# Holding back the weight queue of a decoder step until the small vectors, the identity and x have landed

## The chip, the cores and the metric

The kernel runs on one core of one Trainium2 chip. The metric is the device time of one execution in microseconds (us). Three runs of the kernel before gave 1500.31, 1504.12 and 1505.19 us; the median is 1504.12 us. Each run comes from the same inputs.

## The reference

One decoder layer is computed for a prompt of 256 tokens and for 8 single-token samples, model width 1024, all in 32-bit floats. Cut to what matters:

```
m = silu(c) @ w_mod + b_mod                        # c: 9 vectors; w_mod 1024 x 6144
sh1, sc1, gt1, sh2, sc2, gt2 = split(m, 6)
h = rmsnorm(x, g_pre_mix) * (1 + sc1) + sh1
aq, af, ai, ag, bq, bk, bv, gate_a, gate_b = split(h @ w_in)    # w_in 1024 x 5632
o_a = hgrn2(aq, af, ai, ag)                        # 4 heads, 128x128 state
o_b = differential_attention(bq, bk, bv)           # 4 heads, paged cache for the samples
merged = sigmoid(gate_a) * (o_a @ w_proj_a) + sigmoid(gate_b) * (o_b @ w_proj_b)
x = x + gt1 * rmsnorm(merged @ w_out, g_post_mix)
h2 = rmsnorm(x, g_pre_ffn) * (1 + sc2) + sh2
x = x + gt2 * rmsnorm(moe(h2), g_post_ffn)         # top 4 of 32 experts, 12 MB of weights each
```

## The kernel before, in words

The engines run programs of their own, written out in order by hand and tied together by semaphores. Three of them issue DMAs, each on a queue of its own.

SyncE issues nearly all weights, in the order of the list `UNITS`: 54 pieces of 1 MB that pass through a ring of four slots (tile `ring`). The first eight are pieces of `w_mod` for the first third of the modulation (`("mod", 0, k)`); then each half of a 512-column block of `w_in` is followed by two more `w_mod` pieces for as long as there are any; the branch and output projections come last. Before piece n, from the fifth on, SyncE waits until the piece that had the same slot is used (`after_unit`, L300 to L322). After the ring it issues the weights of expert 0, and then loops over the other experts, twelve pieces each, into the ring and the tile `late`.

ScalarE begins (L890 to L914) by issuing seven small vectors into `vrows` and the 128x128 identity into the head of `cst` (eight DMAs, semaphore `small_loaded`), and then the two parts of x (`x_loaded`, 32 when both are in). It then takes a sigmoid of the conditioning vectors once they are transposed, waits for x, squares its three chunks with a row sum, takes a root and an exponential, and only then issues the rest of the constants table (`cst`, semaphore `cst_loaded`), which is first used in the attention.

GpSimd issues biases, post-norm gains, lambdas and router weights (17 DMAs, L355 to L369), and later the pages of the cache.

TensorE waits for `small_loaded`, transposes `vrows` (`vt`, L455), and VectorE makes silu(c) from it (`cT`, L1120). Then `mod_part` (L466) multiplies the ring pieces as they land, four matmuls in 32-row strips for each piece's 2048 columns (eight instructions in the trace). After the eighth, VectorE adds the bias, four transposes bring the result into columns (`mt0`), and eight rounds follow in which TensorE transposes a 128-column block of the normalised x (`xt0` to `xt7`, L452) and VectorE scales and shifts it into `hT` (L1092). After the last round the first input projection starts (`in_T(4)`, L496). The projections, the two token mixers, the output projection and the router follow, and from about 455 us the loop over experts (L828, L847, L869), for which the weights stream in behind.

Of the kernel before, what the change touches and what calls it, by code (L numbers as in the profile page):

```python
# [132 lines left out]
def build(nc, a, o):  # L133

    ctx = ExitStack()
    with ctx:
# [5 lines left out]
        def S(name):  # L142

            if name not in sems:
                sems[name] = ctx.enter_context(nc.semaphore(name))
            return sems[name]
# [126 lines left out]
        def slot(i):  # L273

            return ring[:, i * SLOT:(i + 1) * SLOT] if i < 4 else late[:, (i - 4) * SLOT:(i - 3) * SLOT]
# [6 lines left out]
        def after_unit(n):  # L282

            u = UNITS[n]
            if u[0] == "mod":
                return "mod_used", KC * u[1] + u[2] + 1
            if u[0] == "in":
                names = IN_NAMES[u[1]]
                if u[2] == 1:
                    return "proj_full", PROJ[names[-1]] + 1  # L290
                return ("proj_full", PROJ[names[1]] + 1) if len(names) == 4 else ("tok_half", 1 if u[1] == 6 else 2)
            if u[0] in ("pb", "pa"):
                return "merge_full", (KC if u[0] == "pa" else 0) + 4 * (u[1] + 1)
            return "yo_full", 2
# [4 lines left out]
        @block.sync  # L299
        def _(sp):  # L300
            wmod = a["w_mod"][0].rearrange("(k p) n -> p k n", p=P)
            win = a["w_in"][0].rearrange("(k p) n -> p k n", p=P)
            for n, u in enumerate(UNITS):
                if n >= 4:
                    sem, value = after_unit(n - 4)
                    sp.wait_ge(S(sem), value)
                dst = slot(n % 4)
                if u[0] == "mod":
                    src = wmod[:, u[2], u[1] * 2048:(u[1] + 1) * 2048]
                elif u[0] == "in":  # L310
                    src = win[:, :, u[1] * 512 + u[2] * 256:u[1] * 512 + (u[2] + 1) * 256]
                    dst = dst.rearrange("p (k n) -> p k n", k=KC)
                elif u[0] in ("pa", "pb"):
                    w = a["w_proj_a" if u[0] == "pa" else "w_proj_b"][0].rearrange("(h p) n -> p h n", p=P)
                    src = w[:, :, u[1] * 512:(u[1] + 1) * 512]
                    dst = dst.rearrange("p (h n) -> p h n", h=H)
                else:
                    src = a["w_out"][0, u[1] * 256:(u[1] + 1) * 256, :].rearrange("(k p) n -> p k n", p=P)
                    dst = dst.rearrange("p (k n) -> p k n", k=2)
                sp.dma_start(dst, src).then_inc(S(f"piece{n % 4}_landed"), 16)  # L320

            def load_expert(e, u):  # L322
                one = slice(e, e + 1) if isinstance(e, int) else bass.ds(e, 1)
                if u < 8:
                    src = a["w_gate_up"][0, one, u * P:(u + 1) * P, :]
                    src = src.rearrange("e p n -> p (e n)")
                    dst = slot(u)
                else:
                    src = a["w_down"][0, one, (u - 8) * 2 * P:(u - 7) * 2 * P, :]
                    src = src.rearrange("e (k p) n -> p (e k) n", p=P)  # L330
                    dst = slot(u).rearrange("p (k n) -> p k n", k=2)
                sp.dma_start(dst, src).then_inc(S(f"w{u}_landed"), 16)  # L332


            sp.wait_ge(S("merge_full"), 2 * KC)
            sp.wait_ge(S("st_stored"), 16)
            for h in range(2):
                sp.wait_ge(S(f"s0_{h}_stored"), 32)
            for u in range(4, 12):
                load_expert(0, u)  # L340
            sp.wait_ge(S("yo_full"), 2)
            for u in range(4):
                load_expert(0, u)
            sp.wait_ge(S("tab_ready"), 1)
            with sp.Fori(1, E) as e:
                before = sp.value_load(used_tab[0:1, bass.ds(e, 1)], min_val=0, max_val=12 * MAXB)
                for u in range(12):

                    sp.wait_ge(S("w_used"), before + (u + 1))
                    load_expert(e, u)  # L350
# [1271 lines left out]
```

## Time and profile before

| | |
|---|---|
| runs | 1500.31, 1504.12, 1505.19 us |
| median | 1504.12 us |
| span of the profiled execution, first to last instruction | 1499.4 us (no other time of that execution is on record) |
| TensorE matmul busy | 1331.5 us, 89% |
| VectorE / ScalarE / GpSimd busy | 390.1 / 196.2 / 56.7 us |
| mean granted TensorE clock | 0.943 |
| DMA | 496.16 MB, mean 331 GB/s |
| share of the SyncE queue (q1) / GpSimd queue (q0) / ScalarE queue (q10) | 76.4% / 4.6% / 2.5% of 16 engines |

Busy time is the time in which an engine executed something; the queue shares are the time of their packets as a part of what the 16 DMA engines have over the span. The granted clock is a part of TensorE's full speed.

### The profile page before, as it was taken

Reading aid. Unit: us, or ns where it says so; the run is one execution under the profiler, and the core shown is the slowest. Engines: PE = TensorE matmul, PEld = TensorE weight load, DVE = VectorE, ACT = ScalarE, POOL = GpSimd, SP = SyncE. Lnnn points to the kernel's source line nnn. Section 1 sums busy time; section 2 is a strip of 40 time slices with the busy share of each in tenths; the row PEclk is TensorE's granted clock in tenths of the full one; section 3 lists DMA queues with packets and bytes.
Section 4 is the critical chain, followed back from the end, with each engine's and each line's share of the span. In section 5 each row is a group of like instructions: output and inputs, shape, how many; then the busy total and the mean of one; then the engine's idle time right before and its main releaser. Section 6 shows DMA issues by size and latency. Waiting matters only on the chain.

```text
span 1499.4 us, 18873 instructions
## 1 busy us (share of the span) xinstructions
PE 1331.5 (89%) x6987; PEld 716.6 (48%) x6988; DVE 390.1 (26%) x653; ACT 196.2 (13%) x321; POOL 56.7 (4%) x108
## 2 busy tenths in 40 slices
PE   2999999998868999999899998999999999989980
PEld 0576778876444544544344333544543443334430
DVE  1713652355353211211122111211211121112105
ACT  2001410011121111111011110110110111101111
POOL 2001011100000000000000000000000000000003
PEclk9798999799976999999999999999999999999995
DMA  9888475322721999999999999799999999999974
GB/s 304 299 297 282 140 256 165 119 108 91 280 112 66 397 419 417 417 419 418 419 416 419 418 419 417 293 394 417 419 419 419 416 418 419 420 417 417 419 290 144
DMA packets 114980, 496.16 MB, mean 331 GB/s; under 512 B 9461, under 2 KB 32234, under 8 KB 78954
## 3 DMA queue, kind: packets, MB, share of 16 engines
q1 hardware_dynamic: 101216, 459.30, 76.4%
q0 software_dynamic: 6832, 23.09, 4.6%
q10 hardware_dynamic: 6906, 13.42, 2.5%
q8 instruction: 16, 0.26, 0.1%
q14 instruction: 10, 0.08, 0.0%
HBM read 478.41 MB, written 17.37 MB: 331 GB/s over the span
## 4 chain that ended last, share of the span: by engine, by line
PE 54%; DMA 24%; SPq 12%; DVE 5%; ACT 2%; issue 2%; ACTq 0%; POOL 0%; DVEq 0%; POOLq 0%
DMA late<-in_w_gate_up 21%; PE PB L847 13%; SPq L332 11%; PE PB L869 9%; PE PB L828 8%; PE PB L496 8%; PE PB L513 2%; PE PB L758 2%; PE PB L725 2%; PE PB L466 1%; PE PB L678 1%; PE PB L452 1%; PE PB L521 1%; DMA cst<-in_consts 1%; DVE wide L1099 1%
## 5 line engine op out<-in xcount | busy, mean ns | idle before, releaser
L847 PE MATMUL PB<-late,gates 128*64 128x512 f32 x1056 | 245.5, 598 | 37.8 <-DMA late<-in_w_gate_up 37.8
L869 PE MATMUL PB<-late,gates 128*64 128x512 f32 x1056 | 233.9, 595 | 24.1 <-ACT gates L1046 24.1
L847 PE MATMUL PB<-ring,gates 128*64 128x512 f32 x1056 | 233.6, 595 | 0.3 <-issue 0.3
L1570 DVE TENSOR_SCALAR gates<-PB 128x512 f32<-128x512 f32 x33 | 22.8, 692 | 740.8 <-PE PB L854 740.8
L828 PE MATMUL PB<-gates,wide 128*128 128x64 f32 x1632 | 194.3, 280 | 6.9 <-DVE gates L1542 6.9
L828 PEld LDWEIGHTS PB<-gates,wide 128*128 128x128 f32 x1632 | 189.7, 196 | 20.6 <-issue 20.6
L847 PEld LDWEIGHTS PB<-late,gates 128*64 128x64 f32 x1056 | 69.3, 136 | 208.3 <-issue 104.5
L496 PE MATMUL PB<-hT,ring 128*128 128x264 f32 x576 | 149.6, 418 | 2.6 <-DVEq L1157 2.2
L869 PEld LDWEIGHTS PB<-late,gates 128*64 128x64 f32 x1056 | 72.9, 137 | 163.9 <-issue 131.9
L847 PEld LDWEIGHTS PB<-ring,gates 128*64 128x64 f32 x1056 | 76.0, 138 | 147.6 <-issue 145.2
L496 PEld LDWEIGHTS PB<-hT,ring 128*128 128x128 f32 x576 | 116.7, 207 | 34.4 <-issue 8.9
L1042 ACT ACTIVATE gates<-gates 128x512 f32<-128x512 f32 x33 | 20.8, 630 | 434.9 <-DVE gates L1570 434.9
L1566 DVE TENSOR_REDUCE gates<-att 128x192 f32<-128x768 f32 x33 | 48.8, 1478 | 50.9 <-PE PB L828 50.9
L1049 ACT ACTIVATE gates<-PB 128x512 f32<-128x512 f32 x33 | 19.7, 597 | 246.8 <-PE PB L876 246.8
L1042 ACT ACT_TABLE_LOAD x33 | 42.3, 1283 | 52.6 <-issue 52.6
L421 POOL CAST sel<-cst 96x64 bf16 x31 | 7.2, 233 | 958.8 <-PE PB L876 958.8
L1044 ACT ACTIVATE gates<-PB 128x512 f32<-128x512 f32 x33 | 19.7, 597 | 133.7 <-PE PB L828 133.7
L466 PE MATMUL PB<-ring,cT 128*32 128x512 f32 x192 | 29.4, 734 | 8.2 <-DMA ring<-in_w_mod 6.5
L725 PE MATMUL PB<-late,ring 128*128 128x264 f32 x128 | 30.8, 403 | 4.3 <-DVE gates L1096 4.3
L1563 DVE TENSOR_TENSOR att<-cst,small 128x768 f32<-128x768 f32 x33 | 31.6, 958 | 1.1
L513 PE MATMUL PB<-ring,hT 128*128 128x256 f32 x128 | 30.8, 396 | 0.0
L725 PEld LDWEIGHTS PB<-late,ring 128*128 128x128 f32 x128 | 25.3, 199 | 10.4 <-issue 5.6
(260 smaller groups left out, 850.1 us busy)
## 6 DMA issues: line engine op xcount, KB each, us to landing
late<-in_w_gate_up SPq DMA_DIRECT2D x128, 1024.0 KB, 23.1
late<-in_w_down SPq DMA_DIRECT2D x128, 1024.0 KB, 22.1
ring<-in_w_gate_up SPq DMA_DIRECT2D x128, 1024.0 KB, 18.7
ring<-in_w_mod SPq DMA_DIRECT2D x24, 1024.0 KB, 7.0
ring<-in_w_in SPq DMA_DIRECT2D x22, 1024.0 KB, 8.5
ybuf<-gates ACTq DMA_DIRECT2D x66, 128.0 KB, 6.2
wide<-in_cache_k POOLq DMA_DIRECT2D x16, 256.0 KB, 3.3
G<-in_cache_v POOLq DMA_DIRECT2D x16, 256.0 KB, 3.0
```

The source lines that it names most:

```text
L332: sp.dma_start(dst, src).then_inc(S(f"w{u}_landed"), 16)
L466: mm = pe.matmul(PB[4][32 * j:32 * j + 32, :], cT[:, k, :], w[:, j * 512:(j + 1) * 512], start=(k == 0), stop=(k == KC - 1))
L496: mm = pe.matmul(bank[:, 0:T], w[:, k * 256 + (j % 2) * P:k * 256 + (j % 2 + 1) * P], hT[:, k, :], start=(k == 0), stop=(k == KC - 1))
L513: mm = pe.matmul(banks[c][:, half * 256:(half + 1) * 256], hT[:, k, c * P:(c + 1) * P], w[:, k * 256:(k + 1) * 256], start=(k == 0), stop= ...
L725: mm = pe.matmul(PB[i % 4][:, 0:T], w[:, h * 512 + (s % 4) * P:h * 512 + (s % 4 + 1) * P], src[:, h, :], start=(h == 0), stop=(h == H - 1))
L758: mm = pe.matmul(PB[2 * c + i][:, :], gaT[:, s, c * P:(c + 1) * P], wo[s // 2][:, (s % 2) * D + i * 512:(s % 2) * D + (i + 1) * 512], star ...
L828: mm = pe.matmul(PB[3][:, k * M:(k + 1) * M], xn[:, c, k * P:(k + 1) * P], mo["Pm"][:, c * M:(c + 1) * M], start=(c == 0), stop=(c == NCH ...
L847: mm = pe.matmul(PB[i][64 * half:64 * half + 64, :], mo["xT"][:, k * M:(k + 1) * M], slot(k)[:, i * D + half * 512:i * D + (half + 1) * 51 ...
L869: mm = pe.matmul(PB[2][64 * half:64 * half + 64, :], mo["actT"][:, (k % 4) * P + (k // 4) * M:(k % 4) * P + (k // 4) * M + M], slot(8 + k ...
L1042: act.activation(mo["sig"], mo["glu"], ACT.Sigmoid, scale=ALPHA).then_inc(S("sig_ready"), 1)
L1563: dve.tensor_tensor(eq3, iota, g3, ALU.is_equal).then_inc(S("eq_ready"), 1)
L1566: dve.tensor_reduce(P3, eq_sum, AX, ALU.add).then_inc(S("P_ready"), 1)
```

## The change

SyncE gets two waits. Before its first piece it waits for all eight small transfers of ScalarE's queue (seven vectors and the identity), and before its third piece for both parts of x. Order, sizes and destinations of all DMAs stay as they were.

```
         def _(sp):
             wmod = a["w_mod"][0].rearrange("(k p) n -> p k n", p=P)
             win = a["w_in"][0].rearrange("(k p) n -> p k n", p=P)
+            sp.wait_ge(S("small_loaded"), 16 * 8)
             for n, u in enumerate(UNITS):
+                if n == 2:
+                    sp.wait_ge(S("x_loaded"), 32)
                 if n >= 4:
                     sem, value = after_unit(n - 4)
                     sp.wait_ge(S(sem), value)
```

## Rows read from the trace of the kernel before

**Rows 1.** Chain of waits in order of time: start us, us, what.
```profile
4.66 14.82 DMA cst<-in_consts
21.63 5.27 PE PB L466 x32
26.92 11.53 DMA ring<-in_w_mod
51.01 9.63 PE PB L496 x32
```
**Rows 2.** Windows: length, busy (instructions) of five engines, clock, DMA share, GB/s.
```profile
5.00:10.00 5.00, 0.00 (x0) 0.00 (x0) 0.00 (x0) 1.28 (x1) 5.00 (x10) 1.00 1.00 330
20.00:25.00 5.00, 3.37 (x20) 0.83 (x24) 1.05 (x5) 0.26 (x1) 0.00 (x0) 1.00 1.03 255
35.00:40.00 5.00, 3.81 (x20) 0.40 (x16) 0.69 (x1) 0.00 (x0) 0.00 (x0) 0.50 1.03 407
450.00:480.00 30.00, 22.76 (x86) 15.77 (x87) 12.81 (x36) 4.10 (x9) 0.23 (x1) 0.52 0.01 2
```
**Rows 3.** Waits of TensorE, 51 to 460 us: total us, times, longest.
```profile
PE PB L496 <- DMA ring<-in_w_in: 0.4, 1, 0.4
PE PB L751 <- DMA ring<-in_w_out: 5.1, 1, 5.1
```
**Rows 4.** Timeline of TensorE and VectorE after the eighth piece: start us, us.
```profile
38.49 1.94 PE L466 MATMUL PB<-ring,cT 128*32 128x512 f32 x8 [0.64 <-DMA ring<-in_w_mod]
49.78 0.55 DVE L1092 TENSOR_SCALAR hT<-PB,A,SH 128x256 f32<-128x256 f32 x1 [0.15 <-DVE hT L1096]
```
**Rows 5.** DMA issues: KB each, median us to landing.
```profile
ring<-in_w_mod SPq DMA_DIRECT2D x1, 1024.0 KB, 5.2
wide<-in_cache_k POOLq DMA_DIRECT2D x4, 256.0 KB, 3.1
```
**Rows 6.** Timeline of the ScalarE and GpSimd issues.
```profile
4.66 0.36 ACTq L899 DMA_DIRECT2D cst<-in_consts  x1
5.05 0.50 ACTq L900 DMA_DIRECT2D x<-in_x_prompt  x1
10.40 0.61 POOL L369 DMA_DIRECT2D br<-in_b_router  x1
27.93 1.06 ACT L909 ACTIVATE hT<-x 128x1024 f32<-128x1024 f32 x1 [7.16 <-DMA x<-in_x_sample]
34.60 0.35 ACTq L914 DMA_DIRECT2D cst<-in_consts  x1
```
**Rows 7.** DMA queues, 0 to 9 us: packets, MB, share of 16 engines.
```profile
q1 hardware_dynamic: 277, 2.10, 65.2%
q0 software_dynamic: 94, 0.22, 10.8%
```
**Rows 8.** DMA queues, 0 to 38.5 us.
```profile
q1 hardware_dynamic: 1511, 8.76, 65.0%
q0 software_dynamic: 720, 1.72, 18.5%
q10 hardware_dynamic: 602, 1.37, 13.7%
```
**Rows 9.** DMA queues, 30 to 38.5 us.
```profile
q1 hardware_dynamic: 778, 3.37, 97.2%
q10 hardware_dynamic: 16, 0.18, 5.6%
```
**Rows 10.** TensorE on weight pieces: timeline, then windows (busy, clock, DMA share, GB/s).
```profile
30.94 1.26 PE L466 MATMUL PB<-ring,cT 128*32 128x512 f32 x8 [4.09 <-DMA ring<-in_w_mod]
33.43 1.93 PE L466 MATMUL PB<-ring,cT 128*32 128x512 f32 x8 [1.23 <-DMA ring<-in_w_mod]
22.00:24.00 2.00, 2.00 (x12) 1.00 0.99 238
24.00:25.00 1.00, 1.00 (x12) 1.00 1.05 221
```
**Rows 11.** Timeline of the second half of the first projection (the first: rows 1).
```profile
62.42 7.39 PE L496 MATMUL PB<-hT,ring 128*128 128x264 f32 x32
```

More of the change, by code:

```diff
@@ L302, in _ @@
             win = a["w_in"][0].rearrange("(k p) n -> p k n", p=P)
+            sp.wait_ge(S("small_loaded"), 16 * 8)
             for n, u in enumerate(UNITS):
+                if n == 2:
+                    sp.wait_ge(S("x_loaded"), 32)
                 if n >= 4:
```

## The prediction

> **What bounds the kernel now.** I read the chain of waits first, from its start. It opens with a wait for the identity matrix, issued at 4.66 us and landed 14.82 us later; then the first four weight pieces are multiplied in one go (5.27 us), then 11.53 us go to weight pieces that land one by one until 38.45 us, and the first projection starts at 51.01 us [rows 1]. The windows table comes second: between 5 and 50 us the DMA share is 1.00 to 1.04 in each of nine stretches of 5 us (three of them stand), so the DMA engines have no free moment there, and TensorE is busy 3.37 us of 5 at 20 to 25 us and 3.81 of 5 at 35 to 40 us [rows 2]. So what sets the time of the eighth weight piece (T7, 38.45 us) is the sum of all packets that pass before it. The early wait for the identity costs TensorE 19.5 us of idleness, and TensorE isn't what is short. From T7 to 51.01 us lie 12.6 us of a fixed sequence: eight matmuls (1.94 us), the bias, four transposes, and eight rounds of transpose and modulation at 0.9 us each on VectorE, the last starting at 49.78 us [rows 4]. From 51 us to the expert loop TensorE's matmuls wait for DMA only twice, 0.4 and 5.1 us (the second for the output weights, whose issue itself waits for TensorE) [rows 3], and at 450 to 480 us the DMA engines stand idle (share 0.01) with the first expert's weights all loaded [rows 2]. A shift of T7 therefore runs through to the end with its full size, in either direction, and no DMA lead absorbs it. My sum is: end = time before + shift of T7 + what the clock does.
>
> **The first wait: when the queue starts.** Before, the first piece was issued at 0.91 us and landed 5.2 us later [rows 5]. After, SyncE stands at its wait with all 54 ring pieces and the expert weights behind it. The last of the eight small transfers, the identity, is issued at 4.66 us [rows 6]. How long it then takes without weights in the way no row shows. From below stand 3.1 us, what 256 KB of cache keys took [rows 5]; from above the 14.82 us of now. I take 3.4, near the lower end, since what it competes with is only GpSimd's queue: small_loaded at about 8, the first weight byte at about 9 instead of 1.9, the first piece at some 14. The second wait, for x (issued at 5.05 us [rows 6], 1 MB), ends at 11 to 12 us; pieces 0 and 1 hold 2 MB, 5 us of traffic from 9 us on, so the third piece is queued before they are through and this wait costs nothing. If x came after 14 us, each us later would cost one.
>
> **Engine time lost while the queue waits.** In the first 9 us the weight queue used 65.2% of the DMA engines, 5.9 us of their time [rows 7]. Those 5.9 us are lost altogether if nothing else can use them, and not lost at all if the other two queues fill them. What they have to fill them with: up to 38.5 us GpSimd's queue takes 18.5%, 7.1 us for 1.72 MB (242 GB/s while it runs), and ScalarE's 13.7%, 5.3 us [rows 8]. GpSimd issues its 1.72 MB until 11.0 us [rows 6], about 180 GB/s on offer, so three quarters of the engines' time from some 3.4 us; from 6 us x fills the rest. That leaves 1.9 to 3.4 us empty and a quarter of 3.4 to 6: 2.2 us lost. Bounds 0 and 5.9.
>
> **What is drawn ahead of T7.** This is the term that I think counts most. The big constants table (1374.5 KB) is issued by ScalarE at 34.60 us, behind x (first square at 27.93 us) and 6.67 us of squares, a root, an exponential and two table loads [rows 6]. By 38.5 us only 0.18 MB of ScalarE's queue since 30 us has passed [rows 9], so nearly all of the table is moved while TensorE and VectorE are in the 12.6 us that follow T7, where DMA isn't needed. With x landed at 11 to 12 us the same steps put the issue at about 19 us, well ahead of T7, and the queues share the engines. 1.41 MB less 0.18 is 1.23 MB; at the rate of the weight queue when it is nearly alone (3.37 MB in 97.2% of 8.5 us, 408 GB/s [rows 9]) that is 3.0 us more before T7. In return the projection weights come that much earlier after T7, and nobody waits for them there. Bounds: 3.0, and 0 if some wait kept the table behind T7, for which I see no cause.
>
> **What less mixing gives back.** Before T7 the weight queue needs 65.0% of 38.5 us, 25.0 us, for 8.76 MB; at 408 GB/s it would be 21.5 [rows 8, 9]. So mixing with the small packets costs it 3.5 us, spread over some 23 us. Now most small traffic passes before the weights or beside the first three, so I take 2.0 of these 3.5 back. x and the small packets may also run faster without weights beside them: at 408 GB/s their 12.4 us for 3.09 MB would be 7.6, so at most 4.8 come back, but small packets are likely slow by themselves (242 GB/s above), so I take 0.8, near the end that changes nothing.
>
> **Sum.** T7 moves by 2.2 + 3.0 - 2.0 - 0.8 = +2.4 us, to about 40.9. From the bounds: 0 + 3.0 - 3.5 - 4.8 = -5.3 (-8.3 if the table too stayed behind T7), and 5.9 + 3.0 - 0 - 0 = +8.9.
>
> **TensorE earlier, and its clock.** The first matmul of the weights moves from 21.63 to some 14 us, worth nothing while T7 is set by DMA: pieces land 2.5 us apart and need 1.94 us at the slow rate [rows 4, 10]. Ring slots come free in time: piece 4 needs piece 0 used, at 16 us. The back-to-back run of 5.2 us, in which the matmuls came to double their rate (12 in 2.00 us from 22 to 24 us, 12 in 1.00 us from 24 to 25 [rows 10]), disappears. Before, it bought nothing: after the idle 4 us the next eight were still fast (1.26 us), the later ones slow (1.93, 1.94) [rows 4, 10], and the granted clock reads 0.50 (1.2 GHz) at 35 to 40 us [rows 2]. Even spacing should end in the same state, so 0. If the clock were high at T7, the last piece saves 1.0 and the first projection 2.2 (9.63 against 7.39 us [rows 1, 11]); the modulation rounds are VectorE's and save nothing: -3.2 at best.
>
> The profiled span is 1499.4 us and the median of the runs 1504.12, so 4.7 us lie around or between executions; none of the change touches these, so I add +2.4 to the median: 1506.5 us.
>
> **What the Trainium skill says against it.** The trace shows first that the identity, 64 KB, took 14.82 us next to the weight stream [rows 1]. "DMA: Bandwidth & Descriptors", section Rules for kernel authors, advises to issue a DMA early and to wait on its semaphore late, so that setup overlaps. By that rule the 7 us of later start would be lost in full, about 1511; by the rows above other queues fill most of them. It is near the slower rival below, which is priced from rows alone.
>
> **The rivals.** A difference of less than 0.3% (4.5 us) can't be told from none here.
> - Slower: the other queues can't use the engines while SyncE waits. What speaks for it: in the first 9 us GpSimd's queue moved only 0.22 MB (10.8% [rows 7]), perhaps because it is slow to start and not because weights were in its way. Then 5.9 are lost, the table costs 3.0, and 2.0 come back with less mixing: +6.9, 1511 us. It decides from the point where the engines stand empty over 4.3 us in total. Chance 0.24.
> - Faster: mixing was the real price, all 3.5 us of the weights and 4 of x and the small packets come back and the clock is high at T7: 2.2 + 3.0 - 3.5 - 4 - 3.2 = -5.5, 1498.6. For it: 255 GB/s at 20 to 25 us against 407 at 35 to 40 [rows 2]. Against it: small packets keep their cost wherever they stand. Chance 0.10.
> - Nothing happens: T7 within 1 us of 38.45 because the DMA queue is only reordered; 1504. A part of my case, as both read as no change.
> - The waits don't delay as said, small_loaded still coming near 19 us because GpSimd's packets and x hold the identity back: all would be late by 10 us. ScalarE's queue sends the identity ahead of x, so I give this 0.01, in slower.
>
> **The numbers.** Forecast 0.65 with its mirror case, slower 0.25, faster 0.10. Time 1506.5; the range reaches up to the slower rival's price and ends below at -3 us, and leaves about 1 in 10 out on either side: 1501 to 1511.
>
> **What would show it.** Right: identity landed near 8 us and the first transpose just behind it; first weight matmul at 13 to 15; the table issued at 18 to 20; DMA share under 0.8 at 0 to 5 us and 1.0 from 6 us on; T7 at 40 to 42; projection 12.6 us later; expert loop shifted by as much. Wrong: T7 below 38 with a rate over 350 GB/s between 10 and 30 us (mixing was underrated); T7 over 43 (engines empty); a table that passes after T7; a granted clock of 1.00 at the first projection.

## The result and the profile after

Over 20 runs each, the changed kernel has a median of 1508.59 us (1501.41 to 1513.06) and the kernel before 1502.39 us (1496.69 to 1508.69). The ratio is 1.0033 with a 95% interval of 1.0019 to 1.0047: slower by 5.0 us, between 2.9 and 7.1. (The ratio is an estimate from all the runs with its interval, and not the quotient of the two medians, which lie 6.2 us apart. Where a gain or loss of the whole kernel is given in us below, it is worked out from such a ratio.) That is on the edge of what I had called no difference; its sign is clear, and it is the sign of the forecast (+2.4 us).

The span of the profiled execution is 1506.6 us. The chain of waits of the kernel after, in order of time (start us, us, what):

```profile
4.92 11.68 DMA x<-in_x_sample
16.99 13.12 DMA ring<-in_w_mod
32.15 9.67 DMA ring<-in_w_mod
41.87 1.98 PE PB L469 x8
54.38 9.39 PE PB L499 x32
```

Against [rows 1], the wait for the identity is gone from the head, and a wait for x and 22.8 us of waits for weight pieces stand there. That the chain passes through x doesn't yet make the wait for x a cause; the first run below takes it out. The eighth piece lands at 41.82 us instead of 38.45 (the end of the second wait for pieces; T7, +3.37 us), and the first projection starts at 54.38 instead of 51.01 us, again +3.37. The 12.6 us between the two are the same.

The timeline of the kernel after has the steps that the prediction dated:

```profile
8.11 0.43 PE L455 MATMUL PB<-cst,vrows 101*128 101x101 f32 x1 [8.11 <-DMA cst<-in_consts]
16.68 1.06 ACT L912 ACTIVATE hT<-x 128x1024 f32<-128x1024 f32 x1 [7.31 <-DMA x<-in_x_sample]
19.74 1.93 PE L469 MATMUL PB<-ring,cT 128*32 128x512 f32 x8 [11.20 <-DMA ring<-in_w_mod]
23.34 0.35 ACTq L917 DMA_DIRECT2D cst<-in_consts  x1
```

The vectors are there at 8.1 us (predicted 8), but x only at 16.7 (11 to 12), the first weight matmul runs at 19.74 (14), and the table is issued at 23.34 (19) instead of 34.60 [rows 6]. TensorE got only 1.9 us of head start out of this, and used none of it. Two more of the listed signs failed: the DMA share is 0.89 at 5 to 10 us, not 1.0 from 6 us on (windows below), and the expert loop doesn't start 3.4 us later but 6.6, as the two timelines of its first matmul say, before and after:

```profile
460.56 10.48 PE L828 MATMUL PB<-gates,wide 128*128 128x64 f32 x48 [6.92 <-DVE gates L1542]
```
```profile
467.19 8.13 PE L831 MATMUL PB<-gates,wide 128*128 128x64 f32 x37 [6.93 <-DVE gates L1545]
```

I come back to this below.

The windows of the kernel after, with the columns of [rows 2]; then the first 5 us of the kernel before:

```profile
0.00:5.00 5.00, 0.00 (x0) 0.01 (x1) 1.48 (x5) 0.00 (x0) 3.75 (x12) 1.00 0.23 65
5.00:10.00 5.00, 0.43 (x1) 0.18 (x1) 0.88 (x5) 1.55 (x2) 5.00 (x10) 1.00 0.89 238
20.00:25.00 5.00, 3.40 (x16) 0.20 (x8) 2.42 (x4) 3.26 (x6) 0.00 (x0) 1.00 1.02 365
35.00:40.00 5.00, 3.60 (x24) 0.36 (x16) 0.00 (x0) 0.00 (x0) 0.00 (x0) 1.00 1.01 421
```
```profile
0.00:5.00 5.00, 0.00 (x0) 0.01 (x1) 1.48 (x5) 0.00 (x0) 3.75 (x12) 1.00 0.60 204
```

The DMA share (last but one) is where the empty time is read. Before, 2.0 us of the first 10 are empty (5 x 0.40, and none from 5 to 10); after, 5 x 0.77 + 5 x 0.11 = 4.4. So 2.4 us were lost by this count, with 2.2 predicted.

The DMA queues of the kernel after, first 38.5 us (packets, MB, share of 16 engines):

```profile
q1 hardware_dynamic: 1040, 7.62, 53.0%
q10 hardware_dynamic: 730, 2.61, 20.0%
q0 software_dynamic: 720, 1.72, 16.9%
```

ScalarE's queue has moved 2.61 MB by then against 1.37 [rows 8]: the 1.24 MB of difference are the table, all of it now ahead of T7, and the weight queue is 1.14 MB behind, about one weight piece.

### The profile page after: what moved, and what is told of

Its sections match the earlier page's. It is cut to its first block, busy times and chain, and to the rows that moved or that the text cites. A ratio compares the mean times of both kernels' runs of the same rounds, so it can differ in the third digit from the quotient of the medians.

```text
span 1506.6 us, 18873 instructions
## 1 busy us (share of the span) xinstructions
PE 1336.4 (89%) x6987; PEld 717.2 (48%) x6988; DVE 390.0 (26%) x653; ACT 196.2 (13%) x321; POOL 57.2 (4%) x108
## 4 chain that ended last, share of the span: by engine, by line
PE 56%; DMA 23%; SPq 12%; DVE 5%; ACT 2%; issue 2%; ACTq 0%; POOL 0%; DVEq 0%; POOLq 0%
DMA late<-in_w_gate_up 19%; PE PB L850 13%; SPq L335 11%; PE PB L872 9%; PE PB L831 9%; PE PB L499 9%; PE PB L516 2%; PE PB L761 2%; PE PB L728 2%; DMA ring<-in_w_mod 2%; PE PB L681 1%; PE PB L469 1%; PE PB L524 1%; PE PB L455 1%; DVE wide L1102 1%
## 5 line engine op out<-in xcount | busy, mean ns | idle before, releaser
L1573 DVE TENSOR_SCALAR gates<-PB 128x512 f32<-128x512 f32 x33 | 22.8, 692 | 741.0 <-PE PB L857 741.0
L499 PE MATMUL PB<-hT,ring 128*128 128x264 f32 x576 | 152.8, 425 | 2.8 <-DVEq L1160 2.2
L1045 ACT ACT_TABLE_LOAD x33 | 42.3, 1283 | 52.7 <-issue 52.7
```

Of the source, the lines that this page charges most:

```text
L499: mm = pe.matmul(bank[:, 0:T], w[:, k * 256 + (j % 2) * P:k * 256 + (j % 2 + 1) * P], hT[:, k, :], start=(k == 0), stop=(k == KC - 1))
L1045: act.activation(mo["sig"], mo["glu"], ACT.Sigmoid, scale=ALPHA).then_inc(S("sig_ready"), 1)
```

## The experiments

My theory after the result: T7 is a sum of DMA engine time, and the delay is 2.4 us of empty engines, plus 3.0 for the table, less some 2.0 given back by less mixing (packets of several queues passing side by side). The rivals put it down to the empty engines alone or to one of the waits. For each run the time is the ratio to the kernel before on the same chip (12 runs against 35, 95% interval). T7 comes from one profile each: the landing that released the last group of eight weight matmuls, which I give by the start of that group. Before it is 38.49 [rows 4], in the changed kernel 41.87.

### One wait at a time

The first wait alone:

```
+            sp.wait_ge(S("small_loaded"), 16 * 8)
             for n, u in enumerate(UNITS):
```

> Theory (T7 is the sum of engine time: about 2.4 us left empty while the queue waits, 3.0 us for a constants table drawn ahead of T7, less about 2 us given back by less mixing): the first wait alone does the whole of this, because all four first pieces then follow it and the DMA engines stay full. Identity landed near 8.1 us, T7 at 41.3 to 42.5, median 3 to 4 us over before. Rival (the second wait makes the delay, since the third piece is held until 16.6 us): T7 back at 38.5 to 39.5 and no difference of the medians.

Timeline of TensorE, last group:

```profile
41.83 1.56 PE L467 MATMUL PB<-ring,cT 128*32 128x512 f32 x8 [0.66 <-DMA ring<-in_w_mod]
```

41.83 against 41.87 with both waits; ratio 1.0018 (1.0001 to 1.0034). The first wait does all of the delay of T7, as the theory said. The first projection starts only 2.5 us later than before here (53.52 us), because the last group took 1.56 us instead of 1.94 and the steps behind it were shorter too.

The wait for x alone:

```
             for n, u in enumerate(UNITS):
+                if n == 2:
+                    sp.wait_ge(S("x_loaded"), 32)
```

> Theory: with two pieces in front x lands at about 17 us, the third piece is issued then; pieces 0 and 1 and the other queues keep the engines full until about 14 us, so up to 1 us goes empty, and the table, issued 6.7 us behind x at about 24 us, passes ahead of T7 (3.0 us). T7 at 40 to 42, median +2 to +3.5 us. Rival (only the empty engines of the first 9 us count, the table doesn't): T7 within 1 us of 38.45.

Timeline of ScalarE's issue and of TensorE's last group:

```profile
28.31 0.35 ACTq L916 DMA_DIRECT2D cst<-in_consts  x1
42.31 1.94 PE L468 MATMUL PB<-ring,cT 128*32 128x512 f32 x8 [0.63 <-DMA ring<-in_w_mod]
```

T7 at 42.3, a little over what was expected, and 1.0022 (1.0005 to 1.0040). x landed at 21.6 us, not 17, so the third piece was held longer and the engines stood empty for 2.1 us (window of 20 to 25 us below), where up to 1 was expected; and the table, issued at 28.31 us, again passes ahead of T7. Behind the first wait the second costs nothing, alone it costs as much as the first, by the same two terms, empty engines and the table.

```profile
20.00:25.00 5.00, 0.00 (x0) 0.00 (x0) 0.00 (x0) 3.30 (x6) 0.00 (x0) 1.00 0.57 168
```

### The table, taken out and put in

Both waits, the table behind T7 (the wait stands in ScalarE's program):

```
+            act.wait_ge(S("mod_used"), KC)
             act.dma_start(cst[:, P:], a["consts"][:, P:]).then_inc(S("cst_loaded"), 16)
```

> Both waits as in the changed kernel, and ScalarE issues the constants table only when all eight first pieces are used. Theory: the table's 1.41 MB leave the stretch ahead of T7, 3.4 us at 408 GB/s, so T7 falls from 41.8 to 38.4 and the first projection from 54.4 to 51.0; median within 1 us of before. Rival (the waits cost by empty engines and by slower landing of the first pieces alone, the table only fills gaps): T7 stays at 41 to 42 and the median 3 to 5 us over before.

```profile
38.90 1.94 PE L469 MATMUL PB<-ring,cT 128*32 128x512 f32 x8 [0.61 <-DMA ring<-in_w_mod]
40.95 0.36 ACTq L918 DMA_DIRECT2D cst<-in_consts  x1
```

In this timeline T7 falls back by 2.97 us, to 0.41 over before, and the ratio is 1.0001 (0.9984 to 1.0018). I had expected 3.4 us for the whole 1.41 MB, so the last group is half a us later than expected. The rival, that the table only fills gaps, is out.

No wait at all, the table issued right behind x:

```
             act.dma_start(x[0:NS, 2, :], a["x_sample"][:, 0, :]).then_inc(S("x_loaded"), 16)
+            act.dma_start(cst[:, P:], a["consts"][:, P:]).then_inc(S("cst_loaded"), 16)
```

> No wait at all, but the constants table issued right behind x. Theory: only the term of the table acts: 1.23 MB more pass ahead of T7, 3.0 us, so T7 moves from 38.45 to about 41.5 and the median by +3 us, with no empty engine time at the start (DMA share 0.60 at 0 to 5 us, 1.0 from then on). Rival (the table doesn't count): T7 at 38.5, median as before.

```profile
5.78 0.35 ACTq L902 DMA_DIRECT2D cst<-in_consts  x1
41.51 1.64 PE L466 MATMUL PB<-ring,cT 128*32 128x512 f32 x8 [1.44 <-DMA ring<-in_w_mod]
```

T7 moves by 3.02 us and the ratio is 1.0025 (1.0010 to 1.0041), 3.8 us: most of what the change costs, without any part of the change. Between them these two runs show the table's term from both sides: 2.97 us for 1.41 MB taken out, 3.02 us for 1.23 MB put in.

The kernel before with the table late (the edit of the first of these two):

> The kernel before, with the constants table issued only when all eight first pieces are used. Theory: only 0.18 MB of it passed ahead of T7 before, so T7 falls by 0.4 us to about 38.0 and the median stays within 1 us of before: the order of before already had the table in the right place. Rival (any load taken from the first 50 us helps): 2 us or more faster.

T7 at 38.31 (-0.2), as good as expected; the ratio, 1.0019 (0.9998 to 1.0039), can't be told from none and has the wrong sign for a gain. The table had been in the right place by itself. Against this run, which has no part of the table ahead of T7 either, the two waits cost 0.6 us of T7 (38.90 to 38.31).

### GpSimd's loads behind T7

Here the post-norm gains, expert biases, lambdas and router weights go behind the eighth piece; the page table and `b_mod` stay:

```
+            pool.wait_ge(S("mod_used"), KC)
             pool.dma_start(bias_f[:, 0:2 * D], a["b_gate_up"][0]).then_inc(S("bias_loaded"), 16)
...
+            for j in range(4):
+                g = a["g_post_mix"] if j < 2 else a["g_post_ffn"]
...
```

On the kernel before:

> The kernel before, with GpSimd's loads other than the page table and b_mod (post-norm gains, expert biases, lambdas, router weights: 0.95 MB of its 1.72) issued only when all eight first pieces are used; the table isn't touched. Theory: 0.95 of 1.72 MB at 7.1 us is 3.9 us less ahead of T7; x lands earlier by as much, the table is issued near 31 us instead of 34.6 and gives about half of its 1.23 MB ahead of T7 back, 1.5 us. T7 at 35.5 to 37, median 2 us faster. Rival (small packets only fill gaps between the weights): T7 at 38.5, no difference.

```profile
28.49 0.39 ACTq L916 DMA_DIRECT2D cst<-in_consts  x1
39.94 1.93 PE L468 MATMUL PB<-ring,cT 128*32 128x512 f32 x8 [2.27 <-DMA ring<-in_w_mod]
```

I missed here: T7 is later by 1.45 us though 0.95 MB less passes ahead of it; 1.0016 (0.9995 to 1.0036). One cause is in the timeline above, x lands at 21.8 us and lets the table out at 28.5. The other is in the window of 20 to 25 us of this kernel (busy, clock, DMA share, GB/s):

```profile
20.00:25.00 5.00, 4.49 (x28) 1.00 0.42 125
```

The engines stand empty for 2.9 us. All four ring pieces have landed, TensorE got its vectors only at 18.4 us, and no slot is free. Before, the share was 1.03 there [rows 2], because GpSimd's packets and x filled this hole. So the late start of TensorE had a price that was hidden by the very traffic that I took away.

Without waits, table and later loads behind T7:

> No waits of SyncE, with the table and GpSimd's later loads behind T7. Theory: 38.45 - 0.4 - 3.9 = 34.2 us for T7, median 4 us faster than before, if the 2.3 MB that now pass behind T7 don't hold up the first projection weights (needed 12.6 us after T7, landed 6.3 us after it before). Rival (they do, or the later loads reach VectorE late): T7 as said, but the first or second projection starts late and the median is within 1 us of before.

The timeline's last group, then the window:

```profile
36.27 1.68 PE L468 MATMUL PB<-ring,cT 128*32 128x512 f32 x8 [0.56 <-DMA ring<-in_w_mod]
20.00:25.00 5.00, 4.12 (x28) 1.00 0.41 112
```

T7 is 2.2 us earlier instead of 4.2, with the same hole of 3 us, and the ratio is 1.0006 (0.9988 to 1.0024).

With both waits, table and later loads behind T7, run twice:

> Both waits, with the table and GpSimd's later loads behind T7. Theory: with less to pass while the queue waits, the engines stand emptier (some 4 us instead of 2.4 in the first 9 us); T7 at 38.85 - 3.9 + 1.6, 36 to 37, median 2 us faster than before and slower than the next kernel. Rival (the waits are a gain once nothing gets in ahead): T7 under 34.5, the fastest of the four.

> The kernel with both waits and with table and later loads behind T7 once more, beside the three others on one chip. Theory: T7 at 32.5 to 33.5 as the first time, 3 to 4 us faster than before, slower than the kernel that sends the identity ahead. Rival (the first result was chance): within 1 us of before.

The last groups of the two, each from its own timeline, with the window of 20 to 25 us of the second:

```profile
33.02 1.93 PE L471 MATMUL PB<-ring,cT 128*32 128x512 f32 x8 [0.71 <-DMA ring<-in_w_mod]
```
```profile
32.15 1.07 PE L471 MATMUL PB<-ring,cT 128*32 128x512 f32 x8 [1.00 <-DMA ring<-in_w_mod]
20.00:25.00 5.00, 3.85 (x20) 1.00 1.01 423
```

The first time I had expected 36 to 37 and got 33.0: the waits that cost in the changed kernel gain 3.2 us of T7 here (33.02 against 36.27 without them). Ratios 0.9975 (0.9955 to 0.9994) and 0.9968 (0.9947 to 0.9989), 3.8 and 4.8 us faster than before, and so faster than both kernels. With the next one it is the fastest version of this study.

### Which part of this is the wait's

The first wait alone, with the late loads:

> The first wait alone, with the table and GpSimd's later loads behind T7. Theory (what the waits buy is that TensorE is ready when the first pieces land, so that the ring never stands full with idle DMA engines; the wait for x is idle): as with both waits, first weight matmul at 15 to 16.5 us, DMA share 1.0 from 10 us on, T7 at 32.5 to 33.5, median 3 to 4 us faster than before. Rival (holding the third piece for x is part of the gain, as x and the vectors land undisturbed): T7 later by 1 us or more.

T7 at 31.94, ratio 0.9975 (0.9952 to 0.9997): the wait for x is idle here too.

No wait, but the two largest vectors' transfers ahead of the weights on SyncE's own queue, with the late loads:

```
+            sp.dma_start(ident, a["consts"][:, 0:P]).then_inc(S("small_loaded"), 16)
+            sp.dma_start(vrows[VC + 8:VC + 72, :],
+                         a["c_sample"].rearrange("a (k p) -> (a k) p", p=P)).then_inc(S("small_loaded"), 16)
             for n, u in enumerate(UNITS):
```

> No wait: SyncE's queue itself carries the identity and the sample vectors ahead of the first piece, ScalarE's the six smaller vectors; table and later loads behind T7. Theory (order is what counts, the empty engines of the wait are pure loss): all small vectors landed at 6 to 9 us, the engines busy from 2.5 us, no gap at 20 to 25 us, T7 some 3 us under the 33.0 of the kernel with both waits, 29.5 to 31; median 5 to 7 us faster than before. Rival (the vectors left on ScalarE's queue still creep between weight packets): first transpose later than 12 us, a gap with DMA share under 0.6 after it, T7 at 32 to 34.

First transpose, second and third groups, last group:

```profile
8.73 0.43 PE L457 MATMUL PB<-cst,vrows 101*128 101x101 f32 x1 [8.73 <-DMA vrows<-in_g_subln]
15.33 1.94 PE L471 MATMUL PB<-ring,cT 128*32 128x512 f32 x8 [2.56 <-DMA ring<-in_w_mod]
20.52 1.94 PE L471 MATMUL PB<-ring,cT 128*32 128x512 f32 x8 [3.26 <-DMA ring<-in_w_mod]
32.90 1.93 PE L471 MATMUL PB<-ring,cT 128*32 128x512 f32 x8 [1.44 <-DMA ring<-in_w_mod]
```

The vectors land early, no hole opens, and yet T7 is 32.9, not 29.5 to 31, with a ratio of 0.9984 (0.9961 to 1.0006). In the first 10 us the engines stand empty for 2.8 us here and for 4.0 in the second run with both waits (shares 0.44 and 1.00 against 0.26 and 0.93), but T7 is 0.75 us later, not 1.2 earlier. My sentence that the empty engines of the wait are pure loss failed. The windows of 10 to 15 us say why, first this kernel, then the one with both waits:

```profile
10.00:15.00 5.00, 1.94 (x8) 1.00 1.04 300
```
```profile
10.00:15.00 5.00, 0.25 (x4) 1.00 0.98 382
```

With weights, x and `b_mod` all under way the engines are as full and move 300 GB/s; with `b_mod` done and x nearly so, 382. What the wait loses in empty engines it gets back in rate. The packets of the weight queue get slower themselves. In this kernel at 10 to 15 us, and in the one with both waits at 15 to 20 us, when nothing else passes:

```profile
q1 hardware_dynamic: 109, 0.76, 54.5%
```
```profile
q1 hardware_dynamic: 291, 2.12, 100.8%
```

That is 0.40 against 0.28 us of engine time for a packet. The number of active queues isn't it: with weights and the big table side by side (changed kernel, 25 to 30 us; the two queues take 58.9% and 40.8% of the engines) next to nothing is lost.

```profile
25.00:30.00 5.00, 2.15 (x12) 0.20 (x8) 0.00 (x0) 0.00 (x0) 0.00 (x0) 1.00 1.00 417
```

No run separates what x and `b_mod` have that the table hasn't. They come in smaller packets (of all packets 227 of 320 are under 8 KB in this kernel at 10 to 15 us, and 19 of 247 in the stretch with the table); that this is the cause is my guess and isn't shown.

The same order on the kernel before, nothing late:

> The kernel before with only that order: identity and sample vectors ahead of the first piece on SyncE's queue, table and GpSimd's loads as before. Theory: T7 is the sum of packets, which stays; TensorE starts 10 us earlier for nothing, x isn't earlier by much, so the table stays mostly behind: T7 at 37.5 to 39.5, median within 1.5 us of before. Rival (an early start of TensorE is worth something by itself): T7 under 37.

```profile
31.09 0.36 ACTq L915 DMA_DIRECT2D cst<-in_consts  x1
43.27 1.94 PE L469 MATMUL PB<-ring,cT 128*32 128x512 f32 x8 [1.03 <-DMA ring<-in_w_mod]
```

In this timeline T7 is 4.8 us later, ratio 1.0045 (1.0025 to 1.0066), the slowest of all. I had expected 37.5 to 39.5. x lands 3.5 us earlier than before and lets the table out at 31.09, so that nearly all of it passes ahead of T7, worth 3.0 us by the two runs on the table. The whole delay can be counted in the time of the packets up to T7 (0 to 43.23 us):

```profile
q1 hardware_dynamic: 1675, 8.79, 62.8%
q10 hardware_dynamic: 506, 2.51, 16.6%
q0 software_dynamic: 720, 1.72, 15.6%
```

Against [rows 8] SyncE's packets take 2.1 us more (27.1 to 25.0, for nearly the same bytes), ScalarE's 1.9 more, GpSimd's 0.4 less, and 1.1 us more are empty: together the 4.8 us, within rounding. What comes on top of the table is mostly that the weights ran slower, 324 GB/s in their own engine time against 350. The rival, an early start that is worth something by itself, is out where T7 is a sum of packets.

## Why the prediction was right, point by point

- **What bounds the start.** Right. T7 is set by the packets ahead of it, and a shift of T7 reaches the first projection unchanged (+3.37 both in the changed kernel). From the last group to the first projection it is 12.5 us in all eight traces in which that group took 1.93 or 1.94 us, and 11.2 to 12.2 in the six in which it took 1.06 to 1.82.
- **That the shift runs through to the end with its full size.** Its sign is borne out, its size isn't shown. T7 of +3.4, +3.3, +3.8, +0.4 and +3.0 went with +5.0, +2.7, +3.3, +0.2 and +3.8 us by the ratios. But the eight runs on the other two chips all read 1.0 to 3.2 us above their T7 (table late -0.2 with +2.9, GpSimd late +1.5 with +2.4, both late -2.2 with +0.9, identity ahead alone +4.8 with +6.8, the four others at the end of this section). The eight share two sets of runs of the kernel before, so this may be one offset for each chip. In single traces the shift doesn't hold: in the changed one it is +3.4 us at 262 us (the first matmul on the tile `tok`) and +6.7 at 344 us, where the branch projections start, and the expert loop starts 6.6 us later; with the table early it is +0.1 and +6.8 at these two places, with T7 at +3.0. The prediction held that no DMA lead absorbs a shift, and looked only at DMA; what changes the length of the stretch between, in which TensorE is nearly always busy, stays open.
- **Empty engine time.** 2.2 predicted, 2.4 measured by the windows, 2.8 by the count below. The price of the waits as a whole, empty time less rate regained, is 0.4 us by the run with both waits and the late table, or 0.6 against the kernel before with the table equally late.
- **The table.** 3.0 predicted for 1.23 MB, 3.02 measured, and 2.97 for 1.41 MB. This was the main term and it is shown.
- **What less mixing gives back.** I took 2.0 + 0.8 us. T7 came at 41.8 instead of 40.9 us, and which term was 0.9 us off depends on the count. By the windows it is this one: what is left of T7's +3.37 after the two other terms is 2.4 + 3.0 - 3.4 = 2.0. The packets of the changed kernel up to T7 (0 to 41.82 us) say otherwise:

```profile
q1 hardware_dynamic: 1630, 8.88, 56.8%
q10 hardware_dynamic: 730, 2.61, 18.4%
q0 software_dynamic: 720, 1.72, 15.6%
```

Against [rows 8] the weights take 23.8 us, 1.6 less than before for as many bytes; GpSimd's packets take 6.5 instead of 7.1, and ScalarE's without the table's 3.0 us take 4.7 instead of 5.3. That is 2.8 given back, as forecast; empty are 3.8 us instead of 1.1, not 2.2 more but 2.8, and 0.12 MB more of weights (0.3 us) pass. Windows with mixed traffic read shares over 1.00, so the two counts agree no better than to some 0.4 us. The dates missed for one reason that is clear: I let x land at 11 to 12 us as if it ran almost alone, and it took until 16.7 beside GpSimd's packets and two weight pieces. With GpSimd's later loads out of the way it landed at 12.4 us (first square, run with both waits).
- **The second wait.** Right for the changed kernel, for a wrong reason in part: x came after the 14 us beyond which I had said that each us costs one, and it still cost nothing, since GpSimd's and x's packets kept the engines full (share 1.06 and 1.00 at 10 to 15 and 15 to 20 us).
- **TensorE earlier is worth nothing.** Right here, but it holds only while other traffic fills the engines whenever the ring stands full. With that traffic gone the first wait brings T7 forward by 3.2 to 4.3 us (33.02, 32.15 and 31.94 against 36.27).
- **The clock.** Right for the steps that count: in the changed kernel the last group took 1.94 us as before, the granted clock is 0.50 at 45 to 50 us and the first projection takes 9.39 us, against 9.63 [rows 1]. It was not the same state all along: at 35 to 40 us the clock reads 1.00, before 0.50 [rows 2]. And it isn't safe to put it at nothing: in the trace with the first wait and late loads the last group took 1.06 us, and the first projection came 7.9 us earlier where T7 came 6.5 earlier.
- **The advice to issue early and wait late** (the Trainium skill, "DMA: Bandwidth & Descriptors", Rules for kernel authors). Its price of 7 us isn't seen. A wait on the queue costs what nobody else moves in the meantime, here 2.4 us, less what the traffic behind it gains in rate.
- **Time.** +2.4 predicted, +5.0 measured (2.9 to 7.1), +3.4 of it seen in T7. The other 1.6 us are within the interval, and I can't say whether they are real. The sign was forecast for the reason that the runs show; that the time lies within the range owes something to a wide range, since the forecast itself is half of what came.

What stays open: in the versions with late loads and an early start of TensorE the ratios give 1.5 to 3.2 us less than T7 does (T7 -5.5, -6.3, -6.5 and -5.6 against -3.8, -4.8, -3.8 and -2.4 us). In two of them the second half of the first projection waits 1.0 and 2.0 us for its weights behind the packets moved there. In all four traces part of the lead or all of it is gone before the branch projections, which start at 343.84 us in the kernel before and 3.0 and 1.0 us earlier, 5.9 and 0.5 us later in these; why is open.

## What to carry to other kernels

When the DMA engines are full, a transfer's place matters by what stands ahead of the piece that the path waits for: count the bytes ahead of it, those too that another engine will issue earlier because its own wait ends earlier. Freeing an engine sooner can draw a large transfer that nobody needs yet across the path; a wait in front of that transfer, on the event behind which it is harmless, gives the time back. Before moving filler traffic away, look at what it was hiding. And read a change of a few us at the start from an early landing and from many runs: 300 us later a single trace no longer holds it.

## What was not expected of the hardware

Weights beside x and `b_mod` have a price in rate, not only in turns: 300 GB/s with all three under way against 382 with the others nearly done, at nearly the same share of busy engines, and over 420 with the weights alone. Beside the big table the weights pay next to nothing (417 GB/s in all). In the versions with late loads this price makes the order of small and large transfers nearly neutral (T7 32.90 and 32.15 us); with all loads in place it doesn't (43.27 and 41.87).

Single spans are poor evidence for a change of this size. In the run with the first wait alone SyncE issued the third projection piece 1.75 us later than the kernel before and the first expert piece for the ring 9.7 us later. The issues, first before, then with the wait:

```profile
62.55 0.38 SPq L320 DMA_DIRECT2D ring<-in_w_in  x1
421.87 2.12 SPq L332 DMA_DIRECT2D ring<-in_w_gate_up  x4
200.00:300.00 100.00, 99.35 (x497) 0.86 0.56 187
```
```profile
64.30 0.38 SPq L321 DMA_DIRECT2D ring<-in_w_in  x1
431.61 2.00 SPq L333 DMA_DIRECT2D ring<-in_w_gate_up  x4
200.00:300.00 100.00, 99.38 (x469) 0.82 0.55 183
```

Between the two lies a stretch in which TensorE is busy for over 99% of the time and its granted clock was 0.86 in the one and 0.82 in the other (last rows: busy, clock, DMA share, GB/s). The program is the same there. T7 can be read from one profile, though the two profiles of one kernel differ by 0.9 us in it (33.02 and 32.15); the end only from many runs.
